# A two-block transformer kernel on one core: cross-attention heads in pairs inside the query and output blocks, and the second memory's weights moved in the weight stream

## The reference, cut to what matters

```python
def _cross_attention(h, mem, norm_g, norm_m, w_q, w_kv, qn, kn, w_out):   # 4 heads of 256
    u = _rmsnorm(h, norm_g)
    q = _rmsnorm((u @ w_q).reshape(b, s, CROSS_HEADS, CROSS_DIM), qn)
    ...
    sc = jnp.einsum('bshd,bmhd->bhsm', q, k).astype(jnp.float32) * (CROSS_DIM ** -0.5)
    pr = jax.nn.softmax(sc, axis=-1).astype(v.dtype)
    o = jnp.einsum('bhsm,bmhd->bshd', pr, v).reshape(b, s, d)
    return o @ w_out

def _hier_moe(h, ...):      # router: group, then top 2 of 8 experts in it
    ...
    hid = jax.nn.silu(xb @ w_gate[e]) * (xb @ w_up[e])     # e: 32 experts, 1024 x 512 each
    return hid @ w_down[e]                                 # 512 x 1024

# second block
    kv = rmsnorm(mem, g_mem) @ w_mem_kv                    # second memory: keys 512, values 512
```

## Time and profile before

| what | value |
|---|---|
| median of 3 runs | 992.03 us (991.48 to 992.2) |
| profiled execution, its own time | 993.51 us |
| its span, first to last instruction | 991.6 us |
| TensorE busy | 851.9 us (86%) |
| mean granted TensorE clock | 0.926 |
| chain that ended last | PE 61%, DMA 31% |
| moved by the DMA engines | 294.71 MB, mean 297 GB/s |

### The profile page before, as it was taken

How to read it: one execution, slowest core, us unless ns; L and a number is a source line. 1 busy time by engine, 2 the same in 40 slices (tenths; PEclk the granted TensorE clock), 3 DMA queues, 4 the chain that set the end, 5 groups by cost and what they waited for, 6 DMA issues and landing times.

```text
span 991.6 us, 12845 instructions
## 1 busy us (share of the span) xinstructions
PE 851.9 (86%) x5177; PEld 580.8 (59%) x5177; DVE 470.6 (47%) x936; ACT 326.7 (33%) x553; POOL 23.4 (2%) x35
## 2 busy tenths in 40 slices
PE   8999999989998696857576575858999999999997
PEld 8788888868463141313122131312888899888996
DVE  5788767644412110302103021101877788787695
ACT  5766745642120010100000000001434646455533
POOL 1021010100000000000000000000000000000000
PEclk9999999989999798978868878777999999999999
DMA  8754667879699999999999999999655444454531
GB/s 309 277 170 170 213 237 272 296 299 343 244 429 383 441 418 435 434 427 435 430 431 433 426 430 433 424 437 382 205 180 170 134 165 149 149 164 134 189 132 62
DMA packets 63692, 294.71 MB, mean 297 GB/s; under 512 B 3891, under 2 KB 16917, under 8 KB 54549
## 3 DMA queue, kind: packets, MB, share of 16 engines
q1 hardware_dynamic: 62180, 290.91, 74.8%
q10 hardware_dynamic: 1456, 3.03, 0.8%
HBM read 292.88 MB, written 1.05 MB: 296 GB/s over the span
## 4 chain that ended last, share of the span: by engine, by line
PE 61%; DMA 31%; DVE 2%; ACT 2%; issue 2%; SPq 1%; POOL 0%; POOLq 0%; ACTq 0%; DVEq 0%
PE bank L2703 10%; PE bank L2705 10%; PE bank L2704 10%; DMA uT<-in_down_units 9%; DMA uT<-in_gate_units 7%; DMA uT<-in_up_units 7%; DMA ring<-in_down_units 6%; PE bank L3149 5%; PE bank L2768 5%; PE bank L3172 4%; PE bank L2637 3%; PE bank L2770 2%; PE bank L3121 2%; DMA ring<-in_first_blocks 2%; PE bank L3206 1%
## 5 line engine op out<-in xcount | busy, mean ns | idle before, releaser
L1607 DVE TENSOR_TENSOR ring_rounded<-ring,ring_rounded 128x2048 fp32r<-128x2048 f32 x72 | 165.0, 2291 | 85.2 <-ACT ring_rounded L1029 84.6
L1029 ACT ACTIVATE ring_rounded<-ring 128x2048 fp32r<-128x2048 f32 x71 | 135.9, 1914 | 151.0 <-PE bank L2705 119.0
L3149 PE MATMUL bank<-ring,main 128*32 128x512 f32 x744 | 101.2, 680 | 36.2 <-DMA ring<-in_up_units 34.4
L2705 PE MATMUL bank<-ring_rounded 128*128 128x512 f32 x320 | 124.9, 390 | 0.0
L3172 PE MATMUL bank<-ring,main 128*32 128x512 f32 x352 | 60.0, 843 | 33.7 <-DMA ring<-in_down_units 33.7
L3149 PEld LDWEIGHTS bank<-ring,main 128*32 128x32 f32 x744 | 25.9, 123 | 101.9 <-issue 73.3
L2703 PE MATMUL bank<-ring_rounded,uT_rounded 128*128 128x512 f32 x208 | 82.9, 399 | 0.4 <-DVE ring_rounded L1607 0.2
L2704 PE MATMUL bank<-ring_rounded,uT_rounded 128*128 128x512 f32 x208 | 81.0, 390 | 0.0
L2768 PE MATMUL bank<-stream_pair,ring_rounded 128*128 128x512 f32 x192 | 69.6, 405 | 0.0
L2220 DVE TENSOR_TENSOR normed<-bank,normed 128x512 f32<-128x512 f32 x20 | 13.8, 692 | 116.1 <-PE bank L3206 116.1
L2705 PEld LDWEIGHTS bank<-ring_rounded 128*128 128x128 f32 x320 | 60.1, 188 | 13.0
(11 more groups left out here) (383 smaller groups left out, 1561.1 us busy)
## 6 DMA issues: line engine op xcount, KB each, us to landing
ring<-in_up_units SPq DMA_DIRECT2D x11, 4096.0 KB, 33.5
ring<-in_w_in SPq DMA_DIRECT2D x42, 1024.0 KB, 5.1
ring<-in_down_units SPq DMA_DIRECT2D x10, 4096.0 KB, 30.7
ring<-in_gate_units SPq DMA_DIRECT2D x9, 4096.0 KB, 33.2
main<-in_gate_units SPq DMA_DIRECT2D x4, 3072.0 KB, 31.1
main<-in_down_units SPq DMA_DIRECT2D x3, 3072.0 KB, 31.0
main<-in_up_units SPq DMA_DIRECT2D x3, 3072.0 KB, 30.2
ring<-in_w_ckv SPq DMA_DIRECT2D x8, 1024.0 KB, 5.1
```

The costliest lines, as they stand in the source:

```text
L1029: a.activation(rounded(hi_half(name, h)), raw_half(name, h), ACT.Copy).then_inc(hi_made, 1)
L1607: v.tensor_tensor(rounded(raw), raw, as_f32(hi_half(name, h)), ALU.subtract).then_inc(split_made, 1)
L2705: last = mm(dst, left[1], right[0], start=False, stop=last_one, skip_group_check=True)
L3149: last = mm(expert_bank(2 + part)[on, :], xg3[:, h * (KC // 2) + k, on], expert_piece(j, p, u, e, KC)[:, k, :], start=h + k == 0, stop=h * ...
```

## The change

Cross attention on TensorE: `cross_scores(0)`, the scores of the first pair of heads, stands inside `cq1` ahead of its last token tile. The first pair is turned and multiplied ahead of the second pair's scores; the first half of `co0` stands between the second pair's scores and its turn. The output blocks are made by halves in the order (co0,0), (co1,0), (co0,1), (co1,1), each with its own split of the weights, by a new function `output_half` in place of `moving` and `moving_by_quarters`. ScalarE and VectorE lists follow, and the queries' norm is taken in two parts (`cq0`, `cq1`). The plan of PSUM banks is reordered. SP's transfers into the freed ring places follow the new order. The fillers behind the logits go from 14 to 9. The second memory's keys are made behind `pair(0)` and its values behind the loop; both sets of weights now come into `ahead`, the keys' behind quad 1's down units, the values' ahead of the last pair's units.

```diff
-PSUM_PLAN += ["cqT2", "cqT3", "cs0_0", "cs1_0", "cs0_1", "cs1_1", "cpT0", "cpT1"]
-PSUM_PLAN += ["co_0", "co_1", "cpT2", "cpT3", "co_2", "co_3"]
-PSUM_PLAN += ["co0_0", "co0_1", "co1_0", "co1_1"]
+PSUM_PLAN += ["cs0_0", "cs1_0", "cqT2", "cqT3", "cpT0", "co_0", "cpT1", "co_1", "cs0_1", "cs1_1"]
+PSUM_PLAN += ["co0_0", "co0_1", "cpT2", "cpT3", "co_2", "co_3", "co1_0", "co1_1"]
...
+OUTPUT_HALVES = [("co0", 0), ("co1", 0), ("co0", 1), ("co1", 1)]
...
-        key_weights = ring[:, 0:SLOT].rearrange("p (k n) -> p k n", k=KC)
-        value_weights = ahead[:, :].rearrange("p (k n) -> p k n", k=KC)
+        memory_weights = ahead[:, :].rearrange("p (k n) -> p k n", k=KC)
...
             front = (GROUP - 1) * HALF
             sp.wait_ge(moe.unit_used, 2)
             sp.dma_start(unit_runs(1)[0][:, 2 * HALF:front], gate_w[1, 0, :, 2 * HALF:front]).then_inc(unit_landed[1], 16)
-            sp.dma_start(key_weights, SOURCE["xk2"]).then_inc(key_weights_landed, 16)
             load_quad(0, 1, 1, (1, 2))
             sp.wait_ge(moe.unit_used, UNITS)
             sp.dma_start(unit_runs(1)[0][:, front:], gate_w[1, 0, :, front:]).then_inc(unit_landed[1], 16)
             load_quad(0, 1, 1, (3,))
+            load_quad(0, 1, 1, (4, 5))
             sp.wait_ge(moe.unit_used, UNITS + 1)
-            sp.dma_start(value_weights, SOURCE["xv2"]).then_inc(value_weights_landed, 16)
-            sp.wait_ge(memory_keys_made, 2)
-            load_quad(0, 1, 1, (4, 5))
+            sp.dma_start(memory_weights, SOURCE["xk2"]).then_inc(key_weights_landed, 16)
...
             with sp.Fori(1, LAST_PAIR) as j:
                 load_pair(j, j)
+            sp.wait_ge(memory_keys_made, 2)
+            sp.dma_start(memory_weights, SOURCE["xv2"]).then_inc(value_weights_landed, 16)
...
-            moving("cq1", h1_parts, turn_first_queries)
...
+            def first_cross_scores(h, t):
+                if (h, t) == (1, 1):
+                    wait_turned("ckT")
+                    cross_scores(0)
+
+            moving("cq1", h1_parts, turn_first_queries, first_cross_scores)
...
+            def output_half(name, h, before_last_tile=None):
+
+                w_hi, w_lo = (rounded(y).rearrange("p (k n) -> p k n", k=KC // 2)
+                              for y in (hi_half(name, h), raw_half(name, h)))
+                x_hi, x_lo = parts(coT, lo_a)
+                pe.wait_ge(split_made, split_place(name, h))
+                both_drained(f"co_{2 * h}", f"co_{2 * h + 1}")
+                for t in range(TT):
+                    if t and before_last_tile:
+                        before_last_tile()
...
+            turn_last_queries(0)
+            c_turn(0)
+            c_turn(1)
+            turn_last_queries(1)
+            c_out(0)
+            c_out(1)
+            cross_scores(1)
+            output_half("co0", 0)
+            c_turn(2)
+            c_turn(3)
+            c_out(2)
+            c_out(3)
+            output_half("co1", 0)
+            output_half("co0", 1)
+            output_half("co1", 1, turn_first_rows)
...
-            keep_busy(in_bank("h2T0"), 14)
+            keep_busy(in_bank("h2T0"), 9)
...
-                if in_first_quad(j, 0):
-                    memory_keys()
...
-                    if in_first_quad(j, 0):
-                        memory_values()
...
             pair(0)
+            memory_keys()
             with pe.Fori(1, LAST_PAIR) as j:
                 pair(j)
+            memory_values()
```

More of the change, by code:

```diff
@@ L621, in hi_half @@
                 return main[:, 6400:8448]
-            return ring[:, 2 * SLOT + h * HALF:2 * SLOT + (h + 1) * HALF]
+            at = OUTPUT_HALVES.index((name, h)) % 2 if name in ("co0", "co1") else h
+            return ring[:, 2 * SLOT + at * HALF:2 * SLOT + (at + 1) * HALF]
         def quarter(x, q):
@@ L813, in _ @@
             load_staged(3)
+            wait_used(sp, "co0", 0)
+            load_whole(1, 0, gate_w)
             wait_filled(sp, "co_3")
@@ L1026, in split_hi @@
                         wait_filled(act, "xpT3")
+                    elif (name, h) in OUTPUT_HALVES[1:]:
+                        wait_used(act, *(("cq1", 1), ("co0", 0), ("co1", 0))[OUTPUT_HALVES.index((name, h)) - 1])
                     elif n:
@@ L1279, in _ @@
             c_exps(0)
-            c_exps(1)
+            last_queries_out(1)
             c_turned(0)
             c_turned(1)
-            split_hi("co0", [1])
+            for c2 in (2, 3):
+                query_hi(c2)
             co_hi(0)
             co_hi(1)
+            split_hi("co1", [0])
+            c_exps(1)
             c_turned(2)
             c_turned(3)
+            split_hi("co0", [1])
             co_hi(2)
             co_hi(3)
-            split_hi("co1")
+            split_hi("co1", [1])
             for c2 in (0, 1):
@@ L2072, in _ @@
             pair_weights("c", 1, c_prob)
+            split_lo("co0", [0])
+            for c2 in (2, 3):
+                query_lo(c2)
+            query_means(1)
+            co_lo(0)
+            co_lo(1)
+            query_scales(1)
             pair_bias("c", 2, c_neg(2))
@@ L2076, in _ @@
             pair_weights("c", 3, c_prob)
+            split_lo("co1", [0])
             split_lo("co0", [1])
-            for hh in range(4):
-                at = slice(hh * 512, hh * 512 + 512)
-                lo_of(f"co_{hh}", lo_a[:, at], coT[:, at])
+            co_lo(2)
+            co_lo(3)
             NG, NE = N_GROUPS, N_EXPERTS
@@ L2087, in _ @@
             v.memset(top_two[:, :, :], 3e38)
-            add_to_h("co", following=("co1", None))
+            split_lo("co1", [1])
+            add_to_h("co")
             for c2 in (2, 3):
@@ L3056, in c_out @@
                 full(f"co_{hh}", last)
-            for hp in range(2):
-                for hh in (2 * hp, 2 * hp + 1):
-                    c_turn(hh)
-                for hh in (2 * hp, 2 * hp + 1):
-                    c_out(hh)
-            def out_halves(h):
-                both_drained(f"co_{2 * h}", f"co_{2 * h + 1}")
-            moving("co0", parts(coT, lo_a), out_halves)
-            def out_quarter(h, q):
-                if (h, q) == (1, 1):
-                    both_drained("co0_0", "co0_1")
-                    turn(["h2T0", "h2T1"], h_tok)
@@ L3074, in _ @@
-            moving_by_quarters("co1", parts(coT, lo_a), out_quarter)
+            def output_half(name, h, before_last_tile=None):
[3 more added lines that the diff above has]
+                pe.wait_ge(split_made, split_place(name, h))
+                both_drained(f"co_{2 * h}", f"co_{2 * h + 1}")
+                for t in range(TT):
+                    if t and before_last_tile:
+                        before_last_tile()
+                    use, at = f"{name}_{t}", slice(t * P, (t + 1) * P)
+                    dst = (in_bank(use) if h else wait_free(use))[:, :]
+                    for k in range(KC // 2):
+                        one, two = x_hi[:, h * (KC // 2) + k, at], x_lo[:, h * (KC // 2) + k, at]
+                        mm(dst, one, w_hi[:, k, :], start=h + k == 0, stop=False, skip_group_check=True)
+                        mm(dst, one, w_lo[:, k, :], start=False, stop=False, skip_group_check=True)
+                        last = mm(dst, two, w_hi[:, k, :], start=False, stop=h == 1 and k == KC // 2 - 1,
+                                  skip_group_check=True)
+                    if h == 1:
+                        full(use, last)
+                if h == 0:
+                    last.then_inc(half_used, 1)
```

139 lines of the change are left out of this document (56 added, 83 removed).

## The result

The changed kernel takes 986.76 us in the median (984.3 to 988.71, 7 runs), the kernel before on the same chips 992.2 us (991.0 to 994.57, 7 runs). The ratio is 0.9936, 95% interval 0.9917 to 0.9954: faster by 0.6%. Executed again beside the first experiments, on another chip, it took 985.03 us against 993.53 (ratio 0.9930, 0.9914 to 0.9945).

What follows compares the result with a forecast made beforehand. The prediction took the expert weight stream as bound: time of first issue, plus bytes over rate, plus holes. 7.0 + 0.3 + 1.9 = 9.2 us off 993.51 gave 984.3, less 1.5 a median of 982.8 us, range 979.8 to 987.5.

Steps and rivals of the forecast that it cites:

- Cross attention: On TensorE, the new order hides the softmax waits and the slow clock of the value products: 7.0 us gained.
- Output halves, transfers behind the outputs: Outputs by halves cost TensorE nothing; SP's later transfers, 10 us, are hidden before the first expert unit: cost 0.
- rival 4: Late-landing pieces set the first expert units, so cross attention's gain is waited for again: 989.8 us, chance 0.05.
- Fillers: Behind the logits, nine instead of 14: rank counts gain 1.2 us, clock loss at the gather costs 0.9, net 0.3 gained.
- the 1.2 us gained on the rank counts: At the router, nine fillers end 1.7 us sooner, so the rank counts start with VectorE's mark: 1.2 us gained.
- The rule of the Trainium skill: At the router, an idle array falls to 1.2 GHz; by this alone, removing fillers is worth -0.6 us.
- The hole in the weight stream: At 307.20 to 309.30 us in the experts, moving the second memory's keys closes the hole: 1.9 us gained.
- Values: Second memory's values behind the loop: next unit used at T + 40.9, queue dry at T + 44, spare 3 us, cost 0.
- rival 3: The value product, with another 5.27 us of issue, runs the queue dry ahead of the last pair: 985.1 us, chance 0.10.
- Keys: Second memory's keys behind quad 1 have more than the values' 3 us to spare, so no cost.
- Rivals 2 and 5: 2: softmax wait remains in cross attention, 987.3 us, chance 0.12; 5: keys and values at 1.2 GHz, 999.1 us, chance 0.05.

Runs made afterwards that it cites:

- Cross alone: The changed kernel with the second memory's weights, keys and values as before and 14 fillers: 985.32 us, ratio 0.9921 to the kernel before.
- fillers moved: The changed kernel without fillers behind the logits, nine put ahead of the second memory's keys instead: 986.31 us, ratio 0.9933 to the kernel before.
- scores behind: The changed kernel with the first pair's scores behind `cq1`'s last token tile instead of ahead of it: 988.24 us, ratio 0.9951 to the kernel before.
- cover behind: The changed kernel with the first half of `co0` behind the second pair's value products: 990.86 us, ratio 0.9978 to the kernel before.
- 14 + 3: The changed kernel with 14 fillers behind the logits and three more ahead of the last output transposes: 985.27 us, ratio 0.9926 to the kernel before.
- no fillers: The changed kernel with no fillers behind the logits instead of nine: 991.32 us, ratio 0.9985 to the kernel before.
- values between: The changed kernel with 14 fillers and the second memory's values made between quad 6 and quad 7: 985.3 us, ratio 0.9917 to the kernel before.
- values twice: The changed kernel with the second memory's value products made twice over, same result: 996.56 us, ratio 1.0036 to the kernel before.

## Why the prediction was right, and where its steps were off

- **Cross attention**, forecast 7.0, measured 7.6 (R, 240.07 to 232.46), or 7.5 from the first queries' transposes on. Against the two other profiles with the old order it is 6.8, so the forecast lies among the measurements. The mechanism is shown by both undone covers. The margin was not as put: 0.4 us to spare was forecast for the first pair, next to none is there.
- **Output halves, transfers behind the outputs**: cost 0, as forecast. Cross alone kept all of R's gain to the median; rival 4 fell.
- **Fillers**, forecast +0.3, about -1.0 in the profiles: the one step that these give the wrong sign. With the new cross attention R to F is 17.8, 17.8, 17.8 and 18.6 with 14 fillers, 18.3 to 20.3 with 9 (five profiles, mean 19.0), 20.1 and 20.3 with none. The first gather took 3.81 us in all six profiles with 14 fillers, 3.96 to 6.24 in the six with 9, 5.01 and 5.16 with none, over both kernels. The step that failed is the 1.2 us gained on the rank counts. It took the fillers' 5.00 us as their length, but that was their length at a fallen clock; where the clock holds they take 3.37 and end ahead of the mark. With 14 the clock, where it fell, was back by the rank counts; with 9 the rank counts or the gather ran in part at 1.2 GHz. The medians do not settle the size: with 14 fillers the changed kernel's interval just overlaps that with 9, without fillers at the router ("fillers moved") its ratio is 0.9933 against 0.9930 with nine, and in the kernel before the interval leaves a loss of 1 us out. The rule of the Trainium skill that the prediction weighed (TensorE: Matmul & The Clock Gate, "Part 1: The HAM clock gate") had the sign of the profiles, with -0.6.
- **The hole in the weight stream**, forecast 1.9, measured 1.6 in the profiled pair. F to E is 434.9 to 435.5 in the three profiles with the memory as before, 433.1 to 433.8 in five with it moved, and 435.3 to 435.7 in three others with it moved ("scores behind", "cover behind", "14 + 3"). So the gain is there, and in some executions it is given back. In "scores behind" and "14 + 3" the queue moved 407 GB/s over the 25 us from F + 35 on, and 390 and 392 over the 15 us from T + 35 on, where the changed kernel's profile has 433 and 429: 1.2 to 1.3 us below 428 GB/s at each place ("cover behind": 415 and 413). What sets these stretches in one execution and not in the next was not tried.
- **Values**, forecast cost 0 with 3 us to spare. The cost was 0 in the profiled run, the spare 0.4. The time of use was right (T + 40.3 against 39.6), in part by luck: the stop behind the values was 7.79 us and not the 5.27 of before, but the copies took 0.7 and not 1.5, and the down unit at T 5.34 and not 6.15. The edge at which the queue runs dry was 2.3 us too late, since the rate falls ahead of it. At 0.4 us a gather at 1.2 GHz is enough for rival 3. Over the 15 us from T + 35 on the queue moved 429 and 434 GB/s in the two profiles that used the unit at T + 40.3 and 40.5, 417 to 423 in the three at 41.0 to 41.3, and 390 to 413 in the three at 41.4 to 41.6 (granted clock 1.00, 0.97 to 0.98, and 0.95 to 0.96); in "14 + 3", at 41.35, it is 356 GB/s from 595 to 599. Rival 3's other stop did appear, in "no fillers", and cost 5.8 us (F to E, 439.47 against 433.66 with fillers moved) and not 2.3.
- **Keys**: nothing seen of a cost of their own; not tried apart.
- **Rivals 2 and 5**: neither wait nor 27.6 us products; the values took 13.75 us in every profile in which they stand once behind the loop.
- **The sum.** Against the profiled pair 9.2 was forecast and 8.3 came: +0.6 cross attention, -1.3 fillers, -0.3 hole. The median was then taken 1.5 us lower, since before's three runs lay that much below its profile. Before's median is 992.2 us over the seven runs that take these three in, and 993.53, 993.25, 993.65 and 992.46 beside the experiments, so three runs did not fix that offset. The point of 982.8 is 4.0 below the measured 986.76: these 1.5, 0.9 of the sum, and 1.6 by which the changed kernel's median lies above its own profiled run. As a ratio 0.9907 was forecast, and both intervals of the changed kernel lie above it (0.9917 to 0.9954, 0.9914 to 0.9945): by medians the gain is 5.4 and 8.5 us, and the point was too good. That 986.76 falls inside the range, 0.7 us from its end, owes something to the width of the range.

What stays open: why the clock falls at the router in one execution and not in the next, what gives the 2 us of the memory's move back in three profiles, and the 1.5 us of "values between". The fastest version measured is the changed kernel with 14 fillers, 983.33 us; its interval against the changed kernel's just overlaps.

## What to carry to other kernels

Softmax between matmuls is hidden by putting independent matmuls of at least its length between scores and their use; count the cover in time, and expect the clock's loss on top of a wait that is left. When a queue of transfers is said to hold so many us, its rate falls some us ahead of the edge, and work placed against it needs that margin, for TensorE at either clock. Judge fillers over several profiles: their length is read at the clock they ran at, and taking instructions out can bring a stop somewhere else in the program. Take the offset between a profile and a median from more than three runs.

## What the runs showed of the hardware

- TensorE stopped for 7.2 to 8.2 us behind the value products in every profile where these stand behind the loop, with one packet of the instruction queue in each of these stops (39 packets in the whole span). Without the values there the stop was 5.27 and 5.37 us. Nine fewer fillers, 360 us earlier in time, brought a second stop of 5.37 us, and nine fillers put elsewhere took it away.
- The same program met the fall to 1.2 GHz at different points: in the last part of the logits in one profile, behind the rank counts in another, 1.06 us apart from R to F.
- A run of 4 MB transfers ends over 5 us (418, 352, 246, 197, 66, 16 GB/s in "values twice"; 352, 262, 164, 41 in "no fillers"), not at once.
